# Start of a fused encoder layer: constants in one load, one table load, per-slot waits, and head sums at other slots

## The reference, cut to what matters

```python
hn = rmsnorm(h, norm1_w[l])                       # x * rsqrt(mean(x*x) + eps) * w, 512 tokens x 1024
proj = hn @ w_in[l]                               # 1024 x 3456: the stage that is changed
att = rmsnorm(neighbourhood_attention(q, k, v, attn_rpb[l]), attn_norm_w[l])
rk = rwkv7_bidir(proj[..., 3 * ATT_W:], ...)      # begins with the shift by one token, below
h = h + jnp.concatenate([att, rk], axis=-1) @ w_o[l]
hn = rmsnorm(h, norm2_w[l])
h = h + moe(hn, ...)                              # top 4 of 32 experts, three quarters of the time
out = rmsnorm(h, final_norm_w)

# in rwkv7_bidir
p = p + mu_prev * (p_prev - p) + mu_next * (p_next - p)
kk = heads(k * k_k)
kk = kk / jnp.maximum(jnp.sqrt(jnp.sum(kk * kk, axis=-1, keepdims=True)), 1e-12)
```

## Time and profile before

| | |
|---|---|
| median of 3 runs | 1755.33 us (1754.34 to 1756.13) |
| the profiled execution, its own time | 1751.99 us |
| its span in the trace | 1750.2 us |
| TensorE busy | 1638.1 us (94%) |
| VectorE busy | 1478.7 us (84%) |
| ScalarE busy | 1104.2 us (63%) |
| mean granted TensorE clock | 0.972 of full |

### The profile page before, as it was taken

The page is one execution under the profiler, slowest core; times in us unless marked ns, Lnnn a source line. Parts: engine busy times, 40 slices in busy tenths (PEclk is TensorE's granted clock), DMA queues, the critical chain, the costliest instruction groups (busy, mean ns, idle before and its releaser), DMA issues. The chain is left out here.

```text
span 1750.2 us, 33830 instructions
## 1 busy us (share of the span) xinstructions
PE 1638.1 (94%) x12587; PEld 1333.0 (76%) x12588; DVE 1478.7 (84%) x1714; ACT 1104.2 (63%) x1081; POOL 207.1 (12%) x132
## 2 busy tenths in 40 slices
PE   5989989888797999999999999999999999999993
PEld 4768777777675688888888888888888888888882
DVE  3576578686585699999999999999999999999994
ACT  4454435343324577777777777777777777777772
POOL 0001011010101111111121111111121112111110
PEclk9999999999796899999999999999999999999997
DMA  5222000010237999999999999999999999999993
GB/s 182 89 72 82 23 21 30 4 27 15 76 138 259 312 376 383 372 372 376 379 376 363 383 376 382 370 374 377 381 376 360 381 374 378 361 382 377 378 366 109
DMA packets 207600, 473.07 MB, mean 270 GB/s; under 512 B 18734, under 2 KB 29436, under 8 KB 207324
## 3 DMA queue, kind: packets, MB, share of 16 engines
q1 hardware_dynamic: 197148, 442.48, 68.6%
q0 software_dynamic: 9792, 27.28, 7.0%
q10 hardware_dynamic: 576, 2.10, 0.3%
HBM read 454.09 MB, written 26.08 MB: 274 GB/s over the span
## 5 line engine op out<-in xcount | busy, mean ns | idle before, releaser
L2086 DVE TENSOR_TENSOR moe_w_lo<-w_raw,moe_w_hi 128x2048 fp32r<-128x2048 f32 x384 | 867.6, 2287 | 50.9 <-ACT moe_w_hi L2082 50.1
L2082 ACT ACTIVATE moe_w_hi<-w_raw 128x2048 fp32r<-128x2048 f32 x384 | 735.6, 1916 | 118.6 <-PE bank L2103 114.6
L2100 PE MATMUL bank<-moe_w_hi,moe_x_hi 128*128 128x512 f32 x1024 | 406.6, 397 | 1.0 <-DVE moe_w_lo L2086 1.0
L2103 PE MATMUL bank<-moe_w_lo,moe_x_hi 128*128 128x512 f32 x1024 | 401.0, 392 | 0.0
L2101 PE MATMUL bank<-moe_w_hi,moe_x_lo 128*128 128x512 f32 x1024 | 400.1, 391 | 0.0
L2103 PEld LDWEIGHTS bank<-moe_w_lo,moe_x_hi 128*128 128x128 f32 x1024 | 192.9, 188 | 41.1
L2100 PEld LDWEIGHTS bank<-moe_w_hi,moe_x_hi 128*128 128x128 f32 x1024 | 193.1, 189 | 40.4 <-DVE moe_w_lo L2086 1.2
L2101 PEld LDWEIGHTS bank<-moe_w_hi,moe_x_lo 128*128 128x128 f32 x1024 | 193.2, 189 | 38.2
L2100 PE MATMUL bank<-moe_w_hi,moe_a_hi 128*128 128x512 f32 x512 | 209.0, 408 | 1.4 <-DVE moe_a_lo L2137 1.4
L2103 PE MATMUL bank<-moe_w_lo,moe_a_hi 128*128 128x512 f32 x512 | 200.3, 391 | 0.0
L2101 PE MATMUL bank<-moe_w_hi,moe_a_lo 128*128 128x512 f32 x512 | 199.4, 389 | 0.0
(11 more groups left out here) (336 smaller groups left out, 2075.9 us busy)
## 6 DMA issues: line engine op xcount, KB each, us to landing
w_raw<-in_expert_w_up SPq DMA_DIRECT2D x512, 512.0 KB, 8.3
w_raw<-in_expert_w_down SPq DMA_DIRECT2D x256, 512.0 KB, 8.6
proj_w_raw<-in_w_in SPq DMA_DIRECT2D x36, 384.0 KB, 3.3
mixer_bias_table<-in_att_bias SPq DMA_DIRECT2D x16, 256.0 KB, 2.7
x<-in_w_o SPq DMA_DIRECT2D x8, 512.0 KB, 5.2
sum_rows<-x SPq DMA_DIRECT2D x5, 512.0 KB, 5.4
x<-in_x ACTq DMA_DIRECT2D x4, 512.0 KB, 4.2
x<-in_x SPq DMA_DIRECT2D x4, 512.0 KB, 4.8
```

What stands on the lines that cost most here:

```text
L2082: act.activation(w_hi[:, j % RING, :], raw[:, j % RAW, :], ACT.Copy).then_inc(hi_w[j % RING], 1)
L2086: eng.tensor_tensor(w_lo[:, j % RING, :], raw[:, j % RAW, :], w_hi[:, j % RING, :].bitcast(F32), ALU.subtract)\
L2100: pe.matmul(out, s_hi[:, k, :], w_hi[:, j % RING, w], start=first, stop=False)
L2103: ins = pe.matmul(out, s_hi[:, k, :], w_lo[:, j % RING, w], start=False, stop=ends)
```

## The change

It has four parts, all inside `in_projection` but for the host layout.

1. The ten vectors are laid out as one array `vectors` on the host, and loaded by one transfer. The identity matrix goes ahead of it, the weights of chunk 0 follow at once; the experts' bias loads go behind the small mixer constants, the large `c_rwkv` table goes behind the weights of chunk 1.
2. A root of a dummy value (`early`) is the first activation. The roots of x stand one Square later in ScalarE's queue. VectorE makes `vec` and the shift weights before its first mean instead of after its last scaled x.
3. ScalarE and VectorE split slots 0 and 1 of chunk 0, then x blocks 0 to 3, slot 2, x blocks 4 to 7, slot 3. Slot s of chunk 0 waits on TensorE for the x blocks that it uses (at least three, which are the banks that it overwrites), not for all eight.
4. On TensorE head sums 0 and 1 stand behind slot 2 of chunk 2, sums 2 and 3 behind slot 2 of chunk 3 (all four were in chunk 3, behind slots 1 and 2), and the first two v turns of chunk 5 behind slot 2 instead of slot 1. ScalarE's squares, roots and v copies move to match.

```diff
@@ block.sync
-            for name, (r, n) in rows.items():
-                sp.dma_start(vrow[r:r + n, :], ext[name]).then_inc(v_in, 16)
             sp.dma_start(ident[:, :], ext["c_ident"]).then_inc(c_in, 16)
-            for g in range(3):
-                sp.dma_start(braw[E * g:E * g + E, :], ext["expert_b_up"]).then_inc(b_in, 16)
-
+            sp.dma_start(vrow[:, :], ext["vectors"]).then_inc(v_in, 16)
...
-                    sp.dma_start(keep["consts"][:, :], ext["c_rwkv"]).then_inc(m_in, 16)
+                    for g in range(3):
+                        sp.dma_start(braw[E * g:E * g + E, :], ext["expert_b_up"]).then_inc(b_in, 16)
+                if i == 1:
+                    sp.dma_start(keep["consts"][:, :], ext["c_rwkv"]).then_inc(k_in, 16)
@@ block.scalar
+            act.wait_ge(e_set, 1)
+            act.activation(early[:, :], early[:, :], ACT.Sqrt)
...
+            x_square(0)
+            for t in range(1, NT):
+                x_square(t)
+                x_root(t - 1)
+            x_root(NT - 1)
...
+            split_w(0, 0)
+            split_w(0, 1)
+            act.wait_ge(vec_ok, 1)
+            for k in range(4):
+                x_part(k)
+            split_w(0, 2)
+            for k in range(4, KD):
+                x_part(k)
+            split_w(0, 3)
...
-                if i == 3:
-                    for p in range(NPAIR):
-                        square(p)
+                if i == 2:
+                    square(0)
+                    square(1)
                 split_w(i + 1, 1)
                 if i == 3:
-                    length(0)
-                    length(1)
+                    square(2)
+                    square(3)
                 split_w(i + 1, 2)
...
+                split_w(i + 1, 3)
+                if i in (2, 3):
+                    length(2 * i - 4)
+                    length(2 * i - 3)
                 if i == 5:
                     natural(0)
                     natural(1)
@@ block.tensor
             def slot(i, s):
                 pe.wait_ge(lo_w[s], i + 2)
+                if i == 0:
+                    pe.wait_ge(lo_x, max(3, 2 * s + 2))
...
-            pe.wait_ge(lo_x, KD)
             for i in range(NCH):
                 slot(i, 0)
                 slot(i, 1)
-                if i == 3:
-                    lengths(0)
-                    lengths(1)
+                slot(i, 2)
...
+                if i in (2, 3):
+                    lengths(2 * i - 4)
+                    lengths(2 * i - 3)
                 if i == 5:
                     for p in range(NPAIR):
                         parts_done(pe, TRV + p)
                     turn_v(0)
                     turn_v(1)
-                slot(i, 2)
...
-                if i == 3:
-                    lengths(2)
-                    lengths(3)
                 slot(i, 3)
```

More of the change, by code:

```diff
@@ L151, in in_projection @@
         rs = sb("rs", [P, NT])
+        early = sb("early", [P, 1])
         vrow = sb("vrow", [nrows, P])
@@ L178, in in_projection @@
         m_in = sem("mixer_consts_in")
+        k_in = sem("masks_in")
+        e_set = sem("early_set")
         v_in = sem("vectors_in")
@@ L249, in _ @@
             sp.wait_ge(b_out, 16)
+            sp.wait_ge(k_in, 16)
         @block.scalar
@@ L255, in _, with x_square @@
                 act.dma_start(x[:, t, :], xd[:, t, :]).then_inc(x_in[t], 16)
-            for t in range(NT):
+            act.wait_ge(e_set, 1)
+            act.activation(early[:, :], early[:, :], ACT.Sqrt)
+            def x_square(t):
                 act.wait_ge(x_in[t], 16)
@@ L319, in exps, with x_part @@
                 act.activation(Gn[:, z, 0:NCK - 1], mid[:, z, NCK:2 * NCK - 1], ACT.Exp, scale=-KAPPA)
[L321 to L324, removed]
+            def x_part(k):
                 act.wait_ge(turned, k + 1)
@@ L340, in _ @@
                     sigmoids("w", sg, "w0")
-                if i == 3:
-                    length(2)
-                    length(3)
+                if i in (6, 7):
+                    exps(i - 6)
+                split_w(i + 1, 3)
+                if i in (2, 3):
+                    length(2 * i - 4)
+                    length(2 * i - 3)
                 if i == 5:
@@ L389, in _ @@
         def _(dve):
[L390 to L396, removed]
+            dve.memset(early[:, :], 1.0).then_inc(e_set, 1)
             dve.wait_ge(vt, 1)
@@ L408, in _ @@
             dve.tensor_tensor(keepw[:, A:NTILE], keepw[:, A:NTILE], nextw[:, A:NTILE], ALU.subtract).then_inc(shw, 2)
+            for t in range(NT):
+                dve.wait_ge(sumsq, t + 1)
+                dve.tensor_scalar(rs[:, t:t + 1], ss[:, t:t + 1], 1.0 / D, RMS_EPS, ALU.mult, ALU.add).then_inc(ms_done, 1)
+                dve.wait_ge(root, t + 1)
+                dve.reciprocal(rs[:, t:t + 1], rs[:, t:t + 1]).then_inc(rstd, 1)
+                dve.wait_ge(rstd, t + 1)
+                dve.tensor_scalar(x[:, t, :], x[:, t, :], rs[:, t:t + 1], None, ALU.mult).then_inc(xn_done, 1)
             def split_w(i, s):
@@ L429, in other_parts, with x_part @@
                                              in1=dst[:, 0:T - 1], op0=ALU.mult, op1=ALU.add).then_inc(B.free_sem(key), 1)
-            for s in range(NS):
-                split_w(0, s)
-            for k in range(KD):
+            def x_part(k):
                 dve.wait_ge(hi_x, k + 1)
[L435 to L438, removed]
+                dve.scalar_tensor_tensor(out=x_lo[:, k, :], in0=psum[k][:, :],
+                                         scalar=vec[:, rows["norm1_w"][0] + k:rows["norm1_w"][0] + k + 1],
+                                         in1=x_hi[:, k, :].bitcast(F32), op0=ALU.mult, op1=ALU.subtract).then_inc(lo_x, 1)
+            split_w(0, 0)
+            split_w(0, 1)
+            for k in range(4):
+                x_part(k)
+            split_w(0, 2)
+            for k in range(4, KD):
+                x_part(k)
+            split_w(0, 3)
             def rest_of_bias(g, casts):
@@ L547, in _ @@
             pe.wait_ge(c_in, 16)
-            pe.wait_ge(v_in, 16 * len(rows))
+            pe.wait_ge(v_in, 16)
             pe.transpose(psum[0][:, 0:nrows], vrow[:, :], ident[0:nrows, 0:nrows]).then_inc(vt, 1)
@@ L601, in _ @@
                 slot(i, 1)
-                if i == 3:
-                    lengths(0)
-                    lengths(1)
+                slot(i, 2)
+                if i == 1:
+                    pe.wait_ge(m_in, 16 * 5)
+                    pe.wait_ge(lora_act, 1)
+                    lora("w", w2s, DW)
+                if i in (2, 3):
+                    lengths(2 * i - 4)
+                    lengths(2 * i - 3)
                 if i == 5:
@@ L2691, in lay_out @@
                                 "expert_w_down", "expert_b_down")}
-    ext.update({n: lines(a[n]) for n in ("norm1_w", "norm2_w", "attn_norm_w")})
-    ext.update({n: lines(a["rwkv_" + n]) for n in ("mu_prev", "mu_next", "w0", "a0", "k_k", "k_a", "r_k")})
+    vectors = [lines(a[n] if n in ("norm1_w", "norm2_w", "attn_norm_w") else a["rwkv_" + n]) for n in vec_rows()[0]]
+    ext["vectors"] = np.concatenate(vectors, axis=0)
     ext.update({n: a["rwkv_" + n].reshape(P, C) for n in ("w2", "a2", "g2")})
```

9 lines of the change are left out of this document (1 added, 8 removed).

## The result

The changed kernel takes 1742.58 us in the median of four runs (1741.16 to 1744.42), against 1755.20 (1754.34 to 1756.13) for the kernel before: 12.6 us less, a ratio of 0.9937 with a 95% interval of 0.9920 to 0.9954. The forecast was 1744.5, range 1740.5 to 1749.5. The execution profiled after took 1741.16 us, the one before 1751.99: 10.8 less.

The account below looks back on a forecast made before the run. TensorE was taken to bound the projection from 25.5 us on, but for a few waits. −6.8 − 4.7 + 0.7 = −10.8 us gave 1741.2 from the execution's 1751.99, so a median of 1744.5 us, range 1740.5 to 1749.5.

Parts of the forecast that it names:

- The start, −6.8: Projection start: TensorE's first product comes at 18.7 us instead of 25.5, 6.8 us earlier.
- my lower bound of 4: Vectors' landing at the start: taken as 7 us, bounds 4 (nothing ahead of it) and 11.3 (no gain).
- the full second chain: x scaling at the start: Square-to-scale chain twice in a row, 3.0 us where one took 1.5, loss up to 1.5.
- signs, 7 to 8 and 18 to 19.5: Signs at the start: VectorE's copy of the vectors at 7 to 8 us, first product at 18 to 19.5.
- x load 3 delayed by 0.9: Start, by the skill's turn-taking rule: a weight load slips in ahead, first product about 0.9 us later, sum −9.9.
- Late vectors: Rival at the start: vectors come as late as now, first product at 22.7, −6.8 in all, 1748.5 us; 12%.
- a late x load 3: Rival at the start: weights share the engines, the load lands at 12.7, 2 us late; −8.8, 1746.5 us; 10%.
- the gain would not reach the end: Rival in the expert stage: transfers set its pace from some fixed time, so the time stays at 1755 us; 4%.
- Full clock from the first product: Rival at the first products: no products at the low clock level; −12.9, 1742.4 us; 8%.
- The head sums, −4.7: Chunks 2 and 3: excess over the floor 4.2 us instead of 8.9, wait for squares about 0.4 instead of 3.73.
- The v turns, +0.7: Chunk 5: the 0.97 us wait goes, the third turn waits 1.65 us for `natural(0)`; 0.7 us net loss.
- the rival with the price of 2.1: Rival in chunk 5: the new 1.65 us wait drops the clock, costing another 2.1; −8.7, 1746.6 us; 12%.

Follow-up runs that it names:

- experiment 8: The changed kernel with `early` allocated behind all tiles and every slot of chunk 0 waiting for all eight x blocks: 1746.95 us, ratio 0.9965.
- experiment 7: The changed kernel with `early` allocated behind all tiles and the vectors loaded in ten transfers again, behind the identity: 1740.87 us, ratio 0.9929.
- experiments 1 and 12: The changed kernel with `early` allocated behind all other tiles, timed twice: 1742.26 us (ratio 0.9923), then 1739.86 us (0.9927).
- 10: The changed kernel with `early` allocated last and the last two v turns and copies behind slot 0 of chunk 6: 1739.16 us, ratio 0.9924.
- experiment 3: The kernel before with only the new order of head sums and v turns: 1749.83 us, ratio 0.9971.
- 9: The changed kernel with `early` allocated last and each x root right behind its own Square again: 1739.86 us, ratio 0.9926.
- experiment 5: The kernel before with an unused 64-byte tile allocated where `early` stands in the changed kernel: 1752.30 us in one execution.
- experiment 2: The kernel before with an unused 4-byte tile allocated where `early` stands in the changed kernel: 1756.11 us, ratio 1.0004.

## Why the prediction was right, step by step

The time lies in the range, 1.9 us under the forecast, and the parts are those forecast; several sizes were off, and one term was missing.

**The start, −6.8: measured −7.7.** The vectors came at 4.6, near my lower bound of 4 and not at the 7 that I took. Two terms followed: VectorE was free early, so Square 3 waited for nothing but its load (10.31 for 10.75), and the lag of the roots cost less than the full second chain. From Square 3's end I added 3.0 us and it took 2.45 (11.37 to 13.82). From the last scaled x to the first product I had 3.9, and it was 3.95. So the vectors (5.00 for the copy) and the first product both came a little before the times that I had named as signs, 7 to 8 and 18 to 19.5. Of the gain, the slot-wise wait makes 4.0 (experiment 8); that the ten small transfers had been a delay is shown in one trace by experiment 7. The single table load and the order of the splits were not tested by themselves. The −7.7 also hangs on the trace of before. The five traces with the old start have their first product at 23.43 to 25.60 (the identity in at 9.18 to 11.34), the seven with the one load and the slot-wise wait at 17.01 to 17.92. So this part gives 5.5 to 8.6 us by the execution. The three at 23.4 to 23.7 are those with an unused tile; whether that is chance no run shows. The Trainium skill (DMA: Bandwidth & Descriptors, "Queues, rings and completion order") has engines take turns between queues; by it I had put the vectors at about 6, nearer than my own 7. What I had drawn from it for the weights, x load 3 delayed by 0.9, did not occur. SP's queue (q1) did move packets beside x (q10), here from 4.6 to 7 us, but the load was in by 10.31, for 10.75 before:

```profile
q10 hardware_dynamic: 153, 0.56, 60.2%
q1 hardware_dynamic: 199, 0.30, 37.2%
```

**The rivals at the start.** Late vectors and a late x load 3 did not occur in this trace; the first did in experiment 7, at about the price forecast (first product 22.7 forecast, 21.3 seen). That the gain would not reach the end is refuted: the rest of the program grew by 0.8 us only. Full clock from the first product, to which I gave 8%, occurred in the profiled execution: −2.1. It is no rival that is true or false of the kernel: experiments 1 and 12, the same kernel, differ in it. Three of the nine traces with the early start have it throughout (the changed kernel, 10 and 12), so my 8% was too low. The Trainium skill (TensorE: Matmul & The Clock Gate, "Part 1: The HAM clock gate") says that the count of cold matmuls differs between runs of one kernel, and the traces of 1 and 12 agree, with 8 and none.

**The head sums, −4.7: right.** Sums at 1.88 and 1.98 us per four; a wait of 0.34 in experiment 3, 0.4 forecast. Experiment 3 gives −4.2 for the new order, with the v turns in it, so −4.8 for the sums. The changed kernel has no wait there at all, since its slots are longer: another −0.3, which is part of the price of the slower products given back.

**The v turns, +0.7: measured +0.5.** The wait is 1.48 us, 1.65 forecast, in place of 0.97, and it is for `natural(0)` as said. The clock stays up behind it (1.00 from 127 to 135 us): the rival with the price of 2.1 falls.

**What was missing: the products themselves, +2.9.** I costed 648 products as unchanged. In the profiled execution each took 0.0044 us more. Sum: −7.7 − 2.1 − 4.8 − 0.3 + 0.5 + 2.9 = −11.5, the 11.5 of the mixer. So the forecast of 10.8 came close partly by luck: the clock and the spacing, both put at zero, were −2.1 and +2.9. And that the two profiled executions differ by just the 10.8 forecast (1741.2 forecast, 1741.16 measured) is luck too: the mixer came 11.5 earlier, and the rest of the program happened to be 0.8 longer.

**What stays open** is the cause of the spacing. For the place of the tiles: both kernels with a 4-byte tile between x and the weights have 4.20 in every chunk, the eleven traces with weights and x at their old distance have 4.12 from chunk 2 on. Against it: experiments 8 and 9 began at 4.20 with nothing moved, experiment 5 had a level of its own, and the timed runs of experiment 2 show less than the 2.9 us. A spacing that products fall into at the start of a stream and keep until something else interrupts, with the place deciding how easily, would fit these; that experiment 5 comes back to its own level within ten products after every interruption speaks for a larger part of the place than that. No run tests it.

## What to carry to other kernels

An engine works its queue in order, so what counts of a load is the first instruction that waits for it. Ten small transfers in place of one cost 5.3 us until the vectors were in, 3.2 of them for issuing, in the one trace that shows it; the times show nothing of it. Price an idle time of TensorE with its clock: 3.73 us of waiting cost another 1.6 us and more at the low level, 1.48 cost nothing. When a few microseconds matter, read the length of a repeated unit, here a slot, in both traces: a change can leave the order alone and still move all of them. And of a slower engine only what no wait takes up reaches the end.

## What was unexpected of the hardware

Back-to-back products of 512 columns have three spacings at full granted clock, 0.2267, 0.2289 and 0.2333 us. In two executions the spacing changed from 0.2333 to 0.2289 at the first products of another shape, with the tiles where they were. One kernel started its products at the 1.2 GHz level in one execution and at 2.4 GHz in another, 1.6 us apart, after idle times of 2.3 and 2.7 us; the longer one stood before the full clock.
